# The last expert layer computed densely over its whole table instead of by gathered rows

## The reference, cut to what matters

```python
def peer_ffn(h, w_query, sub_keys1, sub_keys2, expert_u, expert_v):
    q = (x @ w_query).reshape(T, 8, 256)
    s1, s2 = q[..., :128] @ sub_keys1.T, q[..., 128:] @ sub_keys2.T     # (T, 8, 128) each
    v1, i1 = top_k(s1, 16);  v2, i2 = top_k(s2, 16)
    top_s, top_p = top_k(v1[..., :, None] + v2[..., None, :], 16)       # of 256 candidates
    e_idx = i1[top_p // 16] * 128 + i2[top_p % 16]
    gate = softmax(top_s)
    # per token c, over its 128 experts e
    act = gelu(einsum('cd,ced->ce', xc, expert_u[e_idx]))
    return einsum('ce,ced->cd', gate * act, expert_v[e_idx])
x = x + gate2 * ff
```

## Time and profile before

| | us |
|---|---|
| median of 3 runs | 4851.69 (4851.02 to 4859.71) |
| the profiled execution, its span | 4850.2 |
| output projection, last layer's normalisation | 4041.84 to 4085.73 |
| queries, routing, gather, fold, store | 4086.03 to the end |
| TensorE busy, whole span | 3687.5 (76%) |
| VectorE busy, whole span | 2582.4 (53%) |
| GpSimd busy, whole span | 1985.1 (41%) |

### The profile page before, as it was taken

The page is one execution under the profiler, slowest core; times in us unless marked ns, Lnnn a source line. Parts: engine busy times, 40 slices in busy tenths (PEclk is TensorE's granted clock), DMA queues, the critical chain, the costliest instruction groups (busy, mean ns, idle before and its releaser), DMA issues.

```text
span 4850.2 us, 35297 instructions
## 1 busy us (share of the span) xinstructions
PE 3687.5 (76%) x10846; PEld 1834.3 (38%) x10846; DVE 2582.4 (53%) x5492; ACT 810.9 (17%) x1937; POOL 1985.1 (41%) x2088
## 2 busy tenths in 40 slices
PE   7779487887677789787795875777778996677777
PEld 2257343454343224441243421221357664322211
DVE  1211567454788434567226674576453333577676
ACT  1110112211111012121101111111231111111111
POOL 0000366554566444466103674466000000576775
PEclk9879799998889999876897998766778997899755
DMA  4235699999999998999647999899200003999999
GB/s 170 87 98 150 214 359 334 356 343 329 359 381 367 347 375 300 328 369 386 215 148 262 352 403 372 336 406 376 70 1 1 1 1 111 327 394 365 409 407 343
DMA packets 482033, 1328.15 MB, mean 274 GB/s; under 512 B 40396, under 2 KB 139980, under 8 KB 481336
## 3 DMA queue, kind: packets, MB, share of 16 engines
q0 software_dynamic: 301824, 1099.07, 59.7%
q1 hardware_dynamic: 173872, 204.09, 12.8%
q10 hardware_dynamic: 6152, 22.74, 1.3%
HBM read 1324.58 MB, written 1.17 MB: 273 GB/s over the span
## 4 chain that ended last, share of the span: by engine, by line
PE 27%; DMA 19%; DVE 6%; POOL 6%; issue 5%; ACT 2%; SPq 1%; ACTq 0%; DVEq 0%; POOLq 0%
PE ps L1444 26%; DMA arena<-in_peer_up,arena 6%; POOL arena L2661 6%; DMA arena<-in_peer_v,arena 4%; DVE arena L717 3%; DMA arena<-in_peer_down,arena 3%; DMA arena<-in_w_mod 2%; DVE arena L730 2%; ACT arena L2125 2%; DMA arena<-in_w_oc 1%; DMA arena<-in_peer_u,arena 1%; SPq L2673 1%; PE ps L1450 1%; DMA arena<-in_ada_w 1%; DMA arena<-mod_scratch 1%
## 5 line engine op out<-in xcount | busy, mean ns | idle before, releaser
L1444 PE MATMUL ps<-arena 128*128 128x512 f32 (+10 forms) x10268 | 3588.4, 501 | 931.7 <-DMA arena<-in_peer_up,arena 318.1
L1444 PEld LDWEIGHTS ps<-arena 128*128 128x128 f32 (+4 forms) x10268 | 1751.5, 197 | 2712.1 <-issue 1469.8
L730 DVE SCALAR_TENSOR_TENSOR arena<-arena,ps 128x1024 f32<-128x1024 f32 x1024 | 1241.2, 1217 | 483.3 <-DMA arena<-in_peer_down,arena 305.9
L2661 POOL DMA_INDIRECT arena<-in_peer_down,arena x768 | 740.7, 964 | 1206.8 <-DVE arena L734 648.9
L2661 POOL DMA_INDIRECT arena<-in_peer_up,arena x768 | 732.2, 953 | 539.3 <-PE ps L1444 367.7
L2125 ACT ACTIVATE arena<-arena 128x128 f32<-128x128 f32 (+5 forms) x1250 | 447.5, 385 | 2158.3 <-PE ps L1444 960.5
L2661 POOL DMA_INDIRECT arena<-in_peer_u,arena x256 | 245.0, 957 | 832.8 <-DVE arena L734 739.5
L730 DVE SCALAR_TENSOR_TENSOR ps<-arena,ps 128x512 f32<-128x512 f32 x508 | 383.3, 754 | 126.7 <-DMA arena<-in_peer_up,arena 90.3
L717 DVE TENSOR_TENSOR arena<-ps,arena 128x512 f32<-128x512 f32 (+3 forms) x198 | 135.5, 684 | 581.4 <-PE ps L1444 553.6
L2125 ACT ACTIVATE arena<-ps 128x512 f32<-128x512 f32 (+3 forms) x345 | 175.1, 508 | 1107.8 <-PE ps L1444 873.6
L2661 POOL DMA_INDIRECT arena<-in_peer_v,arena x256 | 242.3, 946 | 126.1 <-PE ps L1444 81.8
(11 more groups left out here) (33 smaller groups left out, 500.2 us busy)
## 6 DMA issues: line engine op xcount, KB each, us to landing
arena<-in_w_mod SPq DMA_DIRECT2D x24, 2048.0 KB, 15.2
arena<-in_w_in SPq DMA_DIRECT2D x72, 512.0 KB, 10.2
arena<-in_w_in SPq DMA_DIRECT2D x14, 2048.0 KB, 16.4
arena<-in_w_pq SPq DMA_DIRECT2D x12, 2048.0 KB, 10.6
arena<-in_ada_w POOLq DMA_DIRECT2D x24, 1024.0 KB, 5.7
arena<-in_w_out SPq DMA_DIRECT2D x8, 2048.0 KB, 12.9
arena<-mod_scratch ACTq DMA_DIRECT2D x26, 512.0 KB, 8.4
arena<-in_peer_down,arena POOLq DMA_INDIRECT x768, 7.2
```

Source lines behind the costliest of these rows:

```text
L730: self.e.scalar_tensor_tensor(o, a, s, b, op0, op1, accum_out=accum).then_inc(*(inc or self.inc(self.S.vec)))
L1444: return self.e.matmul(o, l, r, start=start, stop=stop)
L2661: self.e.indirect_dma_start(out=o, out_offset=None, in_=table, in_offset=bass.IndirectOffsetOnAxis(ap=idx.bitcast(U32), axis=0)).then_inc( ...
```

## The change

`peer_q`, `gather` and `fold` are replaced for the last layer alone; the other two expert layers keep them. The new order is: queries; then dense dot products of all 256 tokens with all 16,384 experts, with the routing woven in; then the gates, spread over the whole table; then the dense weighted sum; then the addition to X.

- A copy of `expert_u` is laid out by the host in 64 blocks of [128, 2048], so that one block, with d on the partitions, is the transposed stationary operand of 256 experts (`by_columns`). A 128-wide counting row `k3` (0..127) is a new input.
- `queries`: the four weight blocks of 2 MB get buffers of their own (`K.wq`), and are issued right behind the projection's loads. All 16 banks come ahead of any routing.
- `dense_down`: 64 pairs of expert chunks; each is 16 matmuls, 128x128 by 128x256, into one bank, and one gelu of 128x512 by ScalarE into `K.stash[p, c, t]` (expert 128 c + p, token t), 128 KB on each partition. The table streams through four 1 MB buffers (`K.tab`). The routing of both tiles is the weave's back at 2.1 units a step, on the other four banks.
- `choose` does for all 8 heads what `peer_pick` did in pieces, but keeps the two key indices and the gate apart (`K.RT`), and `turn_routes` transposes them, so that `K.RTT[slot, i, t]` has the slots of a token on the partitions.
- `weigh`: for each of 64 groups of 4 tokens GpSimd makes four one-hot tiles of the second index, VectorE four of the first, multiplied by the gate, TensorE multiplies them (four 128x128 by 128x128, one bank), and VectorE multiplies the bank into the stash in place. The stash is read and written at a step of 256 elements.
- `dense_up`: 64 pairs; each is 8 matmuls, 128x128 by 128x512, into four banks that accumulate over all 128 chunks. `expert_v` streams through the same four buffers.
- `add_in`: four bank halves, each a multiplication by the modulation row and an addition to X.

The projection's scratch tile moves in the arena, and it uses two weight slots instead of three.

```diff
-        self.run(self.project(2, 0, K.HT2, area((BG, NB))(512)))
+        self.slot = self.slots["two"]
+        rt = area((K.DR, NB))
+        self.run(self.project(2, 0, K.HT2, rt(512)))
...
-        queries = self.peer_q(2, 0, pt, K.HT2, QA)
-        done = self.until(queries, (0, 0))
...
-        self.weave(self.gather([0, 1], (A["peer_u_2"], A["peer_v_2"]), gelu2, [(2, 0, 5), (2, 0, 5)]),
-                   last_queries(queries), RATE2, done=done)
+        self.run(self.queries(2, K.HT2, QA))
+
+        def routes():
+            for t in range(2):
+                yield from self.route(2, t, pt, QA)
+
+        self.weave(self.dense_down(2, K.HT2, gelu2), routes(), ROUTE)
+        self.ring = self.rings["front"]
+        self.run(self.weigh(2))
+        self.ring = self.rings["back"]
+        self.run(self.dense_up(2, A["peer_v_2"]))
+        self.run(self.add_in(2))
         self.store()
...
@@ class Vector @@
+    def weigh(self, l):
+        K, S = self.K, self.S
+        self.wait_ge(*self.drained(self.turned))
+        self.wait_ge(*self.next(S.count_in, 16))
+        def ones(g):
+            for j in range(4):
+                t = 4 * g + j
+                self.ts(K.WONE[g % 2][:, j, :], K.count, K.RTT[:, 0, t:t + 1], K.RTT[:, 2, t:t + 1], ALU.is_equal, M,
+                        inc=self.inc(S.one_weighted) if j == 3 else None, free=True)
+        ones(0)
+        last = None
+        for g in range(64):
+            b = self.bank()
+            if g == 0:
+                self.wait_ge(*self.drained(self.stashed))
+            if g + 1 < 64:
+                if last:
+                    self.wait_ge(*self.full(last))
+                ones(g + 1)
+            self.wait_ge(*self.full(b))
+            w = K.stash[:, :, 4 * g:4 * g + 4].rearrange("p c t -> p t c")
+            self.tt(w, w, b.ap.rearrange("p (t c) -> p t c", c=128), M, inc=self.drain(b), free=True)
+            last = b
+            yield
...
@@ class Tensor @@
+    def dense_down(self, l, HT, gelu):
+        for n in range(PAIRS):
+            yield
+            b = self.bank()
+            w = K.tab[n % 4].rearrange("p (j k e) -> p j k e", j=2, k=8)
+            self.wait_ge(S.tab_in[n % 4], 16 * (n // 4 + 1))
+            self.wait_ge(*self.vacant(b))
+            for j in range(2):
+                for k in range(8):
+                    i = self.mm(b.ap[:, 256 * j:256 * j + 256], w[:, j, k, :], HT[:, k, :], k == 0, k == 7)
+            i.then_inc(*self.fill(b))
+            self.mark(("table", n))
+    def weigh(self, l):
+        for g in range(64):
+            b = self.bank()
+            self.wait_ge(*self.next(S.one_weighted))
+            self.wait_ge(*self.next(S.one_hot))
+            self.wait_ge(*self.vacant(b))
+            for j in range(4):
+                i = self.mm(b.ap[:, 128 * j:128 * j + 128], K.ONE[g % 2][:, j, :], K.WONE[g % 2][:, j, :], True, True)
+            i.then_inc(*self.fill(b))
+            self.mark(("ones", g))
+            self.weighed = b
+            yield
+    def dense_up(self, l, table):
+        sums = [self.bank() for _ in range(4)]
...
+        for n in range(PAIRS):
+            w = K.tab[n % 4].rearrange("p (j d) -> p j d", j=2)
+            self.wait_ge(S.tab_in[n % 4], 16 * ((n + PAIRS) // 4 + 1))
+            for t in range(2):
+                for j in range(2):
+                    c = 2 * n + j
+                    for hf in range(2):
+                        i = self.mm(sums[2 * t + hf].ap, K.stash[:, c, 128 * t:128 * t + 128], w[:, j, 512 * hf:512 * hf + 512],
+                                    c == 0, c == 127)
...
@@ class Pool @@
+    def weigh(self, l):
...
+        for g in range(64):
+            if g > 1:
+                self.wait_ge(*K.marks["ones", g - 2])
+            for j in range(4):
+                t = 4 * g + j
+                i = self.e.tensor_scalar(K.ONE[g % 2][:, j, :], K.count, K.RTT[:, 1, t:t + 1], None, ALU.is_equal)
+            i.then_inc(*self.inc(S.one_hot))
+            yield
...
@@ class Scalar, dense_down @@
+            if 2 * n + 2 > (K.DR - K.DS) // 256:
+                self.wait_ge(*K.marks["routes", l, 1])
+            self.act(K.stash[:, 2 * n:2 * n + 2, :], b.ap.rearrange("p (c t) -> p c t", t=256), gelu, inc=self.drain(b), free=True)
...
@@ class Sync, dense_down @@
+            if n > 3:
+                self.wait_ge(*K.marks["table", n - 4])
+            self.e.dma_start(K.tab[n % 4], A["down_cols_2"][n]).then_inc(S.tab_in[n % 4], 16)
```

More of the change, by code:

```diff
@@ L30, in const_tables @@
     c["iota"] = np.tile(np.arange(16.0), (128, 1))
+    c["count"] = np.tile(np.arange(128.0), (128, 1))
     def halves(m):
@@ L382, in folded, with queries, route, peer_first @@
         pass
+    def queries(self, l, HT, QA):
+        yield from self.units_of(16)
+    def route(self, l, t, m, QA):
+        for blk in range(4):
+            yield from self.peer_first(l, t, m, QA, blk)
+        yield from self.choose(l, t, m)
+        yield from self.turn_routes(l, t)
+    def peer_first(self, l, t, m, QA, blk):
+        yield from self.units_of(6)
+    def choose(self, l, t, m):
+        yield from self.units_of(17)
+    def turn_routes(self, l, t):
+        yield
+    def dense_down(self, l, HT, gelu):
+        yield from self.units_of(PAIRS)
+    def weigh(self, l):
+        yield from self.units_of(64)
+    def dense_up(self, l, table):
+        yield from self.units_of(PAIRS)
+    def add_in(self, l):
+        yield
     def keys_in(self):
@@ new lines, in turn_routes, with dense_down @@
+    def turn_routes(self, l, t):
+        self.turned = self.bank()
+        yield
+    def dense_down(self, l, HT, gelu):
+        for n in range(PAIRS):
+            yield
+            self.stashed = self.bank()
+    def weigh(self, l):
+        K, S = self.K, self.S
+        self.wait_ge(*self.drained(self.turned))
[19 more added lines that the diff above has]
+            last = b
+            yield
@@ new lines, in dense_up, with add_in @@
+    def dense_up(self, l, table):
+        self.sums = [self.bank() for _ in range(4)]
+        yield from self.units_of(PAIRS)
+    def add_in(self, l):
+        K, S = self.K, self.S
+        self.wait_ge(*self.next(S.gate_in, 16))
+        for t in range(2):
+            for hf in range(2):
+                b, cs = self.sums[2 * t + hf], slice(512 * hf, 512 * hf + 512)
+                tmp = K.stash[:, 4 * t + 2 * hf:4 * t + 2 * hf + 2, :].rearrange("p c t -> p (c t)")
+                xs = self.X(t)[:, cs]
+                self.wait_ge(*self.full(b))
+                self.tt(tmp, b.ap, K.gate[:, cs], M, inc=self.drain(b))
+                self.tt(xs, xs, tmp, AD, inc=self.inc(S.tile_done) if hf else None)
+        yield
@@ new lines, in choose, with turn_routes, dense_down @@
+    def choose(self, l, t, m):
+        yield from self.units_of(17)
+    def turn_routes(self, l, t):
+        K = self.K
+        b = self.bank()
+        self.wait_ge(*self.next(self.S.routes_made))
+        self.wait_ge(*self.vacant(b))
+        self.turn4(b, [(b.ap[:, 128 * i:128 * i + 128], K.RT[t][:, i, :]) for i in range(3)])
+        yield
+    def dense_down(self, l, HT, gelu):
+        K, S = self.K, self.S
+        for n in range(PAIRS):
+            yield
+            b = self.bank()
+            w = K.tab[n % 4].rearrange("p (j k e) -> p j k e", j=2, k=8)
+            self.wait_ge(S.tab_in[n % 4], 16 * (n // 4 + 1))
+            self.wait_ge(*self.vacant(b))
+            for j in range(2):
+                for k in range(8):
+                    i = self.mm(b.ap[:, 256 * j:256 * j + 256], w[:, j, k, :], HT[:, k, :], k == 0, k == 7)
+            i.then_inc(*self.fill(b))
+            self.mark(("table", n))
@@ L2394, in peer_topk @@
         for blk in range(4):
-            yield from self.peer_first(t, m, blk)
+            yield from self.peer_first(l, t, m, None, blk)
         yield from self.peer_pick(t, 0, 8)
@@ L2427, in gather, with queries, choose, turn_routes @@
         self.base += total
+    def queries(self, l, HT, QA):
+        for i in range(16):
+            b = self.bank()
+            self.evict(b, QA[:, i, :], b.ap[:, 0:256])
+            yield
+    def choose(self, l, t, m):
+        K, S = self.K, self.S
+        yield from self.units_of(11)
+        gt = K.RT[t][:, 2, :]
+        self.wait_ge(*self.next(S.route_shift))
+        self.act(gt, gt, ACT.Exp, inc=self.inc(S.route_exp))
+        yield from self.units_of(6)
+    def turn_routes(self, l, t):
+        K = self.K
+        b = self.bank()
+        self.evict(b, K.RTT[:, :, 128 * t:128 * t + 128], b.ap[:, 0:384].rearrange("p (i n) -> p i n", n=128))
+        self.mark(("turned", l))
+        yield
+    def dense_down(self, l, HT, gelu):
+        K, S = self.K, self.S
+        for n in range(PAIRS):
+            yield
+            b = self.bank()
+            self.wait_ge(*self.full(b))
+            if 2 * n + 2 > (K.DR - K.DS) // 256:
+                self.wait_ge(*K.marks["routes", l, 1])
```

(15 more changed lines are left out.)

131 lines of the change are left out of this document (115 added, 16 removed).

## The result

The changed kernel takes 5194.99 us (median of 4 runs, 5184.52 to 5202.77) against 4851.35 us for the kernel before, run beside it: a ratio of 1.0704, 95% interval 1.0688 to 1.072. It is 7% slower, +344 us; the prediction said 5175 us and +323.

What follows compares the result with a forecast made beforehand. It took the last layer's stage to be bound by the DMA rate of 512 gathers of 512 KB. 59.1 + 451.5 + 128.8 + 443.3 + 4.6 = 1087.3 us replace 764.2, +323.1: 5175 us, own range 5120 to 5205 (57%).

Steps and rivals of the forecast that it cites:

- first query matmul starts: Start of the last layer's query matmuls: everything ahead was to stand unchanged, so 4086.03 us as before.
- queries: Query stage: the same 128 matmuls, now together, plus a wait for ScalarE's last eviction; 59.1 us.
- `dense_down`: Down stage: 1024 matmuls of 256 columns at 0.432 us, plus 9.1 us of key products and transposes; 451.5 us.
- `weigh` with its edges: Gate stage: 64 groups at 2.0 us, 128 us, plus 0.8 for the last gelu and first product; 128.8 us.
- `dense_up`, to the last matmul's end: Up stage: 512 matmuls of 512 columns at 0.860 us, plus 3 us for half clock at its start; 443.3 us.
- end: After the last matmul: two instructions stand behind it; 4.6 us.
- The price of a float32 matmul: Dense stages on TensorE: four cycles a column at 2.4 GHz, 0.432 us for 256 columns, 0.860 for 512.
- Rival C: Dense stages: operands pass once, 0.108 us for 256 columns, 4513 us in all; decides from 0.273 us; chance 2%.
- The 3 us for a start at half clock: Start of `dense_up`: 3 us for 6 us of half clock, if the clock fell in `weigh`; `queries` also had 6 us.
- Rival D: Dense stages: the clock does not hold through 440 us of matmuls; at 0.9, 98 us more, 5273 us; chance 4%.
- A: `weigh`: GpSimd and VectorE take turns, or the strided product doubles; about 2.7 us a group, 176 us, 5223 us; chance 22%.
- B: `weigh`: GpSimd sets the pace, 3.8 us a group, 243 us, 5290 us; decides from 0.5 us a comparison; chance 13%.

Runs made afterwards that it cites:

- half_down: The changed kernel with half of the `dense_down` matmuls (4 of 8 products a bank) and all table loads: 4984.17 us.
- bf16_dense: The changed kernel with both dense stages in bfloat16, tables cast while loading, eight half-size buffers instead of four: 4676.97 us, ratio 0.9632 to the kernel before.
- no_reload: The changed kernel loading only the first four of 64 table blocks in each dense stage, all matmuls kept: 5197.59 us.
- flat_product: The changed kernel with the product in `weigh` reading and writing the stash without its 1 KB step (wrong entries weighed): 5197.94 us.
- few_one_hots: The changed kernel with GpSimd making one-hot tiles for the first two groups of `weigh` only, the others reusing them: 5191.19 us.
- the first five experiments: Runs on the changed kernel: half_down, no_reload, flat_product, few_one_hots, and the edits of the last two together (5154.55 us).
- token_major: bf16_dense with the stash laid out token by token, so VectorE reads it without a step, and bfloat16 one-hot tiles: 4616.36 us.

## Why the prediction was right, and where its terms were off

Against its own execution the prediction had 5173.3 us; the changed kernel's has a span of 5195.0, 21.7 more. Term by term:

| term | predicted | measured | off |
|---|---|---|---|
| first query matmul starts | 4086.0 | 4093.7 | +7.6 |
| queries | 59.1 | 56.0 | -3.1 |
| `dense_down` | 451.5 | 450.1 | -1.4 |
| `weigh` with its edges | 128.8 | 149.6 | +20.8 |
| `dense_up`, to the last matmul's end | 443.3 | 440.6 | -2.7 |
| end | 4.6 | 5.1 | +0.5 |

1. **The price of a float32 matmul** decided the case, and held: 0.430 to 0.432 us for 256 columns by the windows, 0.425 by half_down's difference. Rival C (4513 us) had the right price for another type of operand: bf16_dense showed 0.112. That is far under its point of decision, 0.273, and that kernel did come out faster; the point itself was not tried.
2. **Queries, and the clock.** The 3 us for a start at half clock were not due in this execution, neither here nor ahead of `dense_up`: both windows are at 1.00. `weigh` itself has 0.71. In no_reload's execution `dense_up` did start under the full clock and took 1.5 us more, so whether this term is due changes from one execution to the next. Rival D fell with the same rows: 440 us without a pause, at 1.00.
3. **The loads are hidden**: the prediction's argument by rates (152 GB/s wanted, 383 seen) is confirmed by no_reload, 0.1 us off in the down stage, and half_down drew 274 GB/s.
4. **`weigh` is the step that was mis-sized.** The prediction took the low bound for the strided product, 0.692 us; it is 1.284, close to the high bound. It took ScalarE's 0.398 for GpSimd's comparison; it is 0.582 by pace (149.0 us for 256) and 0.609 by the mean record, between that and 0.946. The 0.15 us of handover was not due (TensorE is a group ahead), and VectorE's comparisons cost about as said (1.12 for four, not 1.16). So VectorE needs 2.2 to 2.3 us a group where 2.0 was said, and GpSimd 2.35 where 1.6 was. The product alone adds 0.52 a group (its successor starts 1.21 us after it, 4640.93 to 4642.14), so that the group came out only 0.3 over the forecast is in part luck: the handover and the comparisons took back 0.19. That GpSimd is "hidden under VectorE" was wrong: flat_product shows it setting the pace.
5. **The rivals in `weigh`.** Of A, the nearly doubled product happened and the turns did not (few_one_hots). Its 2.7 a group was too dear: the handover was not due (0.15), the comparisons took 0.04 less, and the product keeps VectorE for 1.21 us and not 1.38. The measured 5195 us lies 20 over the forecast and 28 under A, so the time alone does not tell the two apart; the rows do. B decides from 0.5 us a comparison, as the prediction said, and the measured 0.582 is past that: its mechanism is at work, at 2.35 a group and not at its 3.8. The Trainium skill's rule for A, "SBUF — State Buffer", section Who interferes with whom, was set aside because VectorE's rows are not at a doubled rate; the trace agrees, with 0.005 us on the product and 0.015 on a comparison.
6. **The start.** Ahead of the output projection the compute instructions of before, after and the first five experiments are the same; its first matmul starts at 4041.84 us in the one, 4050.10 in the other, and from 4042.76 to 4053.84 in the experiments. The +7.6 is of that size and not shown to be the change's. It also says how far one execution's span can be trusted: a prediction made against one carries some 10 us that no argument removes.

The sum was right within 21 us of 344 because four fifths of it rest on one price read in three places, and the stage without any row was an eighth of it.

## What to carry to other kernels

Before dense work on TensorE replaces a gather, price it by the type of its operands from a window in which TensorE does not pause: here float32 costs four times bfloat16 (0.43 and 0.112 us for 256 columns), and that decided between 7% slower and 4% faster. Give a strided operand a price of its own, and look at both ends of it: moving the step from reader to writer moved the cost from VectorE to ScalarE. Where two engines share a loop, work out both periods; taking either cost away alone gave 0 to 6 us here, both 45.

## What the runs showed of the hardware that was not expected

- A step between elements costs more than its bytes: the 128x512 product takes 0.69 us contiguous, 1.28 with float32 at a step of 1 KB, 2.65 with bfloat16 at a step of 512 bytes; ScalarE's write of 128x512 goes from 0.60 to 2.77 us with bfloat16 at a step of 256 bytes. The type costs nothing without a step (0.687 us for bfloat16 in token_major). Why bfloat16 with a step pays twice what float32 does stays open: the two differ in the length of the step too.
- A comparison of 128x128 on GpSimd takes 0.59 us with VectorE idle for all but the first 1.1 us (8 in 4.74 us at 4428.06) and 0.58 in `weigh` (256 in 149.0 us), beside VectorE at full load; VectorE's takes 0.34 to 0.39 by the mean record.
- The casting load reads 1 MB and writes half in 2.46 us. By the sizes that is some 430 GB/s read, an estimate, above the 383 GB/s of the plain loads; the 205 GB/s of the window counts what is written.
- TensorE kept a granted clock of 1.00 through 450 us without a pause.
